# Routed experts: another order of the token rows in each gather, and a matrix product with a permutation in place of a transpose

## The reference, cut to what matters

```python
scores = sigmoid(t @ w_router)                     # 264 x 64
e_idx  = top 6 of 64 experts for each token        # 264 * 6 = 1584 choices
gte = einsum('td,edf->tef', t, w_gate_e)           # 1024 -> 256 in each expert
upe = einsum('td,edf->tef', t, w_up_e)
routed = einsum('tef,efd->td', silu(gte) * upe * combine, w_down_e)
```

## Time and profile before

| | us |
|---|---|
| median of three timed runs | 975.01 |
| the profiled execution | 977.85 |
| its span, first to last instruction | 975.4 |
| TensorE busy in the span | 911.1 |
| VectorE busy | 328.6 |
| ScalarE busy | 197.5 |
| GpSimd busy | 154.1 |

### The profile page before, as it was taken

The page is one execution under the profiler, slowest core; times in us unless marked ns, Lnnn a source line. Parts: engine busy times, 40 slices in busy tenths (PEclk is TensorE's granted clock), DMA queues, the critical chain, the costliest instruction groups (busy, mean ns, idle before and its releaser), DMA issues.

```text
span 975.4 us, 18239 instructions
## 1 busy us (share of the span) xinstructions
PE 911.1 (93%) x7483; PEld 565.4 (58%) x7483; DVE 328.6 (34%) x822; ACT 197.5 (20%) x489; POOL 154.1 (16%) x185
## 2 busy tenths in 40 slices
PE   4899999998899789899899999999999999999897
PEld 3688888876566557646655545544445545444442
DVE  0433760046344598436223222121122222111114
ACT  2100110316122189024111111110111111111112
POOL 0000000032475000000132122121211211212110
PEclk9999999998999799999899999999999999999999
DMA  9886675535699548996799999999999999999962
GB/s 372 320 308 255 218 306 196 236 119 219 193 348 338 196 198 282 394 421 264 274 392 403 420 419 422 417 420 422 421 422 415 423 420 420 422 419 423 415 280 93
DMA packets 58916, 325.46 MB, mean 334 GB/s; under 512 B 16177, under 2 KB 25250, under 8 KB 37650
## 3 DMA queue, kind: packets, MB, share of 16 engines
q1 hardware_dynamic: 44930, 305.54, 77.7%
q0 software_dynamic: 12176, 18.56, 5.6%
q10 hardware_dynamic: 1728, 0.18, 0.1%
HBM read 326.65 MB, written 15.81 MB: 351 GB/s over the span
## 4 chain that ended last, share of the span: by engine, by line
PE 42%; DMA 7%; DVE 1%; ACT 0%; issue 0%
PE bank L2232 21%; PE bank L2174 10%; PE bank L2185 6%; DMA ring<-in_w_e 4%; DMA slot_b<-in_w_e 4%; PE bank L2152 3%; PE bank L2264 1%; PE bank L2220 1%; DVE slot_b L2557 0%; DVE slot_b L2565 0%; ACT xt L2346 0%; PE bank L2204 0%; PE bank L2212 0%; DVE hh L2457 0%; ACT sge L2355 0%
## 5 line engine op out<-in xcount | busy, mean ns | idle before, releaser
L368 PE MATMUL bank<-h,ring 128*128 128x264 f32 x672 | 154.6, 391 | 2.4 <-DVE h L244 1.8
L368 PEld LDWEIGHTS bank<-h,ring 128*128 128x128 f32 x672 | 127.9, 192 | 26.6 <-issue 3.0
L2355 ACT ACTIVATE sge<-bank 64x256 f32<-64x256 f32 x64 | 24.1, 377 | 406.2 <-PE bank L2232 406.2
L2457 DVE TENSOR_TENSOR hh<-sge,bank 64x256 f32<-64x256 f32 x64 | 27.1, 423 | 234.9 <-ACT sge L2355 234.9
L2232 PE MATMUL bank<-ring,xt 128*64 128x256 f32 x800 | 96.3, 396 | 4.9 <-DMA ring<-in_w_e 4.1
L2232 PE MATMUL bank<-done_out,xt 128*64 128x256 f32 x832 | 95.5, 382 | 2.0 <-DMA done_out<-in_w_e 2.0
L1563 POOL DMA_INDIRECT xg<-tok_rows,tab_g x32 | 32.0, 999 | 335.7 <-PE bank L2152 323.3
L2398 DVE COPY sq<-bank 128x512 f32<-128x512 f32 x64 | 44.3, 692 | 101.1 <-PE bank L2174 101.0
L2232 PEld LDWEIGHTS bank<-ring,xt 128*64 128x64 f32 x800 | 57.7, 142 | 34.3 <-issue 4.7
L2174 PE MATMUL bank<-ring,ht 128*32 128x512 f32 x320 | 76.4, 598 | 0.0
L2232 PEld LDWEIGHTS bank<-done_out,xt 128*64 128x64 f32 x832 | 57.9, 137 | 29.7 <-DMA done_out<-in_w_e 2.2
(11 more groups left out here) (478 smaller groups left out, 1222.2 us busy)
## 6 DMA issues: line engine op xcount, KB each, us to landing
ring<-in_w_units SPq DMA_DIRECT2D x28, 2048.0 KB, 10.6
done_out<-in_w_e SPq DMA_DIRECT2D x26, 2048.0 KB, 23.1
ring<-in_w_e SPq DMA_DIRECT2D x25, 2048.0 KB, 22.4
slot_b<-in_w_e SPq DMA_DIRECT2D x13, 2048.0 KB, 24.8
ring<-in_w_e SPq DMA_DIRECT2D x20, 1024.0 KB, 23.4
slot_b<-in_w_e SPq DMA_DIRECT2D x11, 1024.0 KB, 25.9
done_out<-in_w_e SPq DMA_DIRECT2D x11, 1024.0 KB, 24.1
row_of<-in_w_e SPq DMA_DIRECT2D x11, 1024.0 KB
```

The source lines that it names most:

```text
L368: mm = pe.matmul(bank[:, t % NB, 0:T], w[:, j, k, :], h[:, k, :], start=(k == 0), stop=(k == KD - 1))
L2355: act.activation(sg[e % 2][:, :], bank[0:LB, 4, 0:FE], ACT.Silu).then_inc(sg_ready, 1)
L2457: dve.tensor_tensor(hh[e % 2][:, :], sg[e % 2][:, :], bank[LB:2 * LB, 4, 0:FE], ALU.mult).then_inc(hh_ready, 1)
```

## The change

1. The permutation of the list in `listed_p`: place n of list l goes to slot 4 * ((n + 4 l) mod 8) + n // 8, where it was 8 * (n mod 4) + n // 4. It is written by eight `tensor_scalar` of 128 x 16 in place of four of 128 x 32.
2. The inner rows are no longer turned by a transpose with the identity but by an ordinary matmul whose second operand is a 64 x 64 permutation matrix `slots`, so the columns leave TensorE in the lists' order.
3. The copy to `ht` becomes a plain one.
4. `slots` is a constant in DRAM (64 x 64 float32), fetched by one more DMA at the head of SP's loop program, into a place that the rotary cosines no longer need. The waits on `comb_in` count 48 instead of 32, and TensorE has one such wait more, before the first turn.

```diff
-                                    for i in range(4):
-                                        ins = dve.tensor_scalar(listed_p[:, i * HB:(i + 1) * HB].rearrange("p (b a) -> p a b", b=4),
-                                                                listed_f[:, :].rearrange("p (a b) -> p a b", b=4),
+                                    for i, c in ((0, 0), (0, 1), (1, 0), (1, 1), (2, 0), (2, 1), (3, 0), (3, 1)):
+                                        lo = i * HB + HB // 2 * ((c + i) % 2)
+                                        ins = dve.tensor_scalar(listed_p[:, lo:lo + HB // 2].rearrange("p (c d) -> p d c", d=4),
+                                                                listed_f[:, :].rearrange("p (d c) -> p d c", c=8)[:, :, 4 * c:4 * c + 4],
...
+                slots = ccol("cos")[0:LB, 0:LB]
...
+                        sp.dma_start(slots, io["slots"]).then_inc(comb_in, 16)
                         sp.dma_start(comb[:, :], io["comb"]).then_inc(comb_in, 16)
...
                             pe.wait_ge(hh_ready, e + 1)
+                            if e == 0:
+                                pe.wait_ge(comb_in, 48)
                             for k in range(2):
-                                mm = pe.transpose(bank[:, 7, k * LB:(k + 1) * LB], hh[e % 2][:, k * P:(k + 1) * P], eye)
+                                mm = pe.matmul(bank[:, 7, k * LB:(k + 1) * LB], hh[e % 2][:, k * P:(k + 1) * P], slots, start=True, stop=True)
                             mm.then_inc(ht_done, 1)
...
-                            dve.tensor_copy(ht[e % 4][:, :, :].rearrange("p k c -> p (k c)").rearrange("p (x a b) -> p x b a", x=4, b=4),
-                                            bank[:, 7, 0:2 * LB].rearrange("p (x b a) -> p x b a", x=4, b=4)).then_inc(ht_ready, 1)
+                            dve.tensor_copy(ht[e % 4][:, :, :], bank[:, 7, 0:2 * LB].rearrange("p (k n) -> p k n", k=2)).then_inc(ht_ready, 1)
...
+    place = np.arange(LB)
+    list_of, n = place // HB, place % HB
+    slot = HB * list_of + 4 * ((n + 4 * list_of) % 8) + n // 8
+    slots = (np.arange(LB)[:, None] == slot[None, :]).astype(np.float32)
```

More of the change, by code:

```diff
@@ L2196, in spread_weights @@
                         def spread_weights():
-                            pe.wait_ge(comb_in, 32)
+                            pe.wait_ge(comb_in, 48)
                             pe.wait_ge(w6_ready, 1)
@@ L2427, in weight_matrix @@
                             if q == 0:
-                                dve.wait_ge(comb_in, 32)
+                                dve.wait_ge(comb_in, 48)
                             if q >= 2:
@@ L2689, in constants @@
     same_row = (r[:, None] % 32 == r[None, :] % 32).astype(np.float32)
-    return {"consts": con, "comb": comb, "same_row": same_row, "rope_row": np.broadcast_to((r[:, None] % ROPE).astype(np.float32), (P, TS * NPG // 4))}
+    place = np.arange(LB)
+    list_of, n = place // HB, place % HB
+    slot = HB * list_of + 4 * ((n + 4 * list_of) % 8) + n // 8
+    slots = (np.arange(LB)[:, None] == slot[None, :]).astype(np.float32)
+    return {"consts": con, "slots": slots, "comb": comb, "same_row": same_row, "rope_row": np.broadcast_to((r[:, None] % ROPE).astype(np.float32), (P, TS * NPG // 4))}
 def kernel(**inputs):
```

## The result

The changed kernel takes 980.43 us (median of 20 runs, 977.69 to 986.16), the kernel before beside it 974.61 us (20 runs). The ratio is 1.0061, 95% interval 1.0045 to 1.0076: slower by 0.6%, inside 1%. The profiled execution takes 978.88 us, its span is 976.7.

A forecast was written before the change was run, and what follows sets the result against it. TensorE and DMA run almost level, DMA falling behind late. Span 975.4 - 11.3 (stalls) + 17.3 (turns) + 0.5 (lists) - 0.1 = 981.8, +2.45 = 984.3 profiled, or 981.4 as median; 982.5 us taken, range 974 to 987.

The forecast's parts named there:

- The turn, +0.27 us per expert: TensorE's turn of the inner rows: four instructions, 0.38 us against 0.11, 17.3 us over 64 experts.
- The pace of L1675: Matmuls with 128 stationary and 64 moving columns, 0.111 us each, taken as the pace of the new turn's four instructions.
- the cheap turn: Rival on TensorE's turn: loads overlap fully, +0.11 us per expert, 7.0 us in all, median 971 to 974; chance 0.13.
- the dear one: Rival on TensorE's turn: +0.33 us per expert or a drain, 21.1 us, median 985 to 988; chance 0.22.
- The stalls gone: Late in the loop, TensorE's 7.8 us of weight waits and 3.5 us of slowed matmuls vanish: 11.3 us back.
- The order buys nothing: The dearer turn alone keeps DMA from ending last, so the gather's order adds nothing beyond the 11.3 us.
- The break-even of 0.17 us per turn: Added turn cost per expert on TensorE under which the changed kernel would be faster than before.
- The sharing over the DMA engines: In the gathers, the new order evens out rows, taking about half of the busiest engine's 6: 15 us over the loop.
- The lists, +0.5 us: Eight half-width `tensor_scalar` in place of four, on the path before the loop: between 0 and 0.6 us more, taken as 0.5.
- The copy to `ht`, 0.1 less: VectorE's plain copy takes 0.3 us against 390 ns; worth 0 in the loop, 0.1 us at the tail.
- The constant and its wait: The DMA for `slots` lands near 483.5, before TensorE's new wait at 486.17: cost 0, or 0.3 us once if late.
- The allowance of 1.1 us for fewer stalls: Timed runs might have fewer DMA stalls to win back than the profile: 982.5 was taken between 981.4 and 984.3.

The follow-up runs named there:

- experiment 2: The changed kernel with the gather's old slot order, so only the turn differs from the kernel before: 981.29 us, ratio 1.006 to the kernel before.
- experiment 5: The kernel before with each turn done twice, four transposes where there were two: 978.04 us, ratio 0.9993 to the kernel before.
- experiment 1: The kernel before with the gather's new order alone, the two transposes kept and three strided copies to `ht`: 968.68 us, ratio 0.992.
- experiment 7: New order, old transposes, tables in slot order, but without the shift of the second tile's lists: 969.46 us, ratio 0.99 to the kernel before.
- experiment 4: The kernel before with lists in plain order, place n in slot n, and a plain copy to `ht`: 985.63 us, ratio 1.009.
- experiment 8: New order, old transposes, tables in slot order, with VectorE's routing weights computed ahead of the loop: 965.22 us, ratio 0.9891 to the kernel before.

## Why the prediction was right

By the steps of the prediction:

- **The turn, +0.27 us per expert.** Measured 0.39 - 0.11 = 0.28 in the chain, and 7.489 - 7.216 = 0.273 in the median step of TensorE. The pace of L1675 carried over to 64 rows, and 0.39 instead of 0.44 fits a first load that hides behind the combining matmul. Both rivals on its size fall, the cheap turn (0.11) and the dear one (0.33). The Trainium skill (TensorE: Matmul & The Clock Gate, table of terms) has float32 four times as fast in transpose mode; the chain shows 0.39 to 0.11, 3.5 times; with nothing hidden the 0.44 of the prediction's upper bound would be 4 times.
- **The stalls gone.** Right for this kernel: none for weights after, no piece of 5.36 us. In the kernel before they begin later than the prediction's "about 45 experts": the first wait of over 1 us comes at 843.5 us, behind 49 experts.
- **The order buys nothing beside this turn.** Right: 1.0061 with it, 1.006 without it (experiment 2). Experiment 5 shows the mechanism by itself: of 7.8 us of added work, within the 11.3 us of stalls, the loop grew by 1.7. The break-even of 0.17 us per turn was not tried; +0.12 (experiment 5) can't be told from the kernel before and +0.27 is slower, which is consistent with it.
- **The sharing over the DMA engines.** Argued ahead. The effect of the order is now shown, and so is that more of the gather's rows move at once in the new order (experiment 1); which engine takes which row is inferred. By the rule of four neighbouring partitions to one engine, with partitions 0 to 31 and 32 to 63 on the same eight, the reference's routing gives the busiest engine 255 rows in the plain order, 210 before, 132 without the shift and 117 in the new order. The waits for weights follow: 17.0, 7.8, 2.7 and 1.8 us, and the ratios 1.009, 1, 0.99 and 0.992. Per row that is (17.0 - 7.8) / 45 = 0.20 and (7.8 - 1.8) / 93 = 0.06 us, above and below the 0.156 of the estimate; that the second is small because few waits were left to remove is argued, not shown. Two other rules fall, by the same count: with partition mod 16 the plain order would be better than the old one (153 rows against 255), and with eight neighbours to an engine the old order would be the best of all (119, against 250 in the plain and 134 in the new order). One rival stays: four neighbours to an engine, but going round all sixteen engines. It gives 255, 210, 129 and 129 in the sequence above, so only the shift could part it from the first rule, and experiment 7 was too close for that. The Trainium skill (DMA: Bandwidth & Descriptors, The descriptor swizzle) states the rule for plain transfers; the gathers of these kernels agree with it as to four neighbours, and no row names an engine.
- **The lists, +0.5 us.** 1.21 - 0.69 = 0.52.
- **The copy to `ht`, 0.1 less.** Measured 291 ns against 390, and nothing waits for it.
- **The constant and its wait.** No wait of TensorE for it appears.
- **The term that was missed.** Two waits came up at the loop's start, 1.2 and 0.5 us, the first for combining weights that come over a chain of DMAs. The sum had no term for them. In the profile before, TensorE came to this point just as the weights did, behind a first step at the lower clock (6.47 us). That step is not the whole reason: in experiment 4 it took 6.59 us and 2.1 us of wait followed. What sets the length of this chain stays open.
- **The number.** 982.5 forecast, 980.43 measured; +6.4 us was the sum in the profile's frame, +5.8 is the difference of the medians. The allowance of 1.1 us for fewer stalls in the timed runs was not needed. In the profile's frame the sum says 984.3 and the profiled execution took 978.88: 5.4 us off, because the loop began 4.6 us earlier and its first step was 2.8 us shorter than in the profile before. The two missed waits stand against that with 1.7 us. The first two are not the change's. The sum of the loop was right; that the forecast of the median came within 2.1 us was helped by luck, since its frame of 2.8 us between the profiled and the median run was a guess.

One figure of the prediction holds only for this change: 11.3 us as what the order alone could give back. With the dear turn all of it came back; experiment 1, without that turn, got 7.3 us, since 1.8 us of waits for weights stay beside TensorE's 7.22 us and a wait of 2.6 us for the combining weights came up.

## What to carry to other kernels

When two resources are both busy to the end, work on one of them is free only up to the time that it now waits for the other; find that sum of waits first, and price every edit against it. Here a fix of the DMA side was paid for with 17 us on TensorE where 11 were to be had, and the same reordering without that payment (make the tables follow the data, rather than turn the data back) wins 0.8%, with the routing weights ahead of the loop 1.1%. Where a gather fetches fewer rows than it has places, try where the filled rows are put: here it moved the kernel by 17 us.

## What was not expected

- The order of rows inside one gather of about 50 rows, 200 KB beside 6 MB of weights in the same two steps, moves a 975 us kernel by 17 us.
- A wait of TensorE of 1 to 3 us near the loop's start goes with a loss on the DMA side: the share falls to 0.72 to 0.86 some ten microseconds later, as experiment 8 shows.
- The loop's start moved between 474.2 and 480.4 us from profile to profile with next to no change to what comes before; a difference of two spans of less than 6 us says nothing until this stretch is taken out.
